# Plain alternation of 512- and 256-column matmuls in every half unit of a two-block kernel

## The reference

```python
h = rms_norm(x, ln_pre_g[layer])
proj = jnp.einsum('bsd,de->bse', h, w_in[layer])                # 2048 -> 18432
rnn_x, rnn_gate, q, k, v, attn_gate, g_rnn, g_attn = split_columns(proj)
hr = rg_lru(rnn_x, ...)                                         # convolution, two gates, scan
y_rnn = jnp.einsum('bsc,cd->bsd', hr * jax.nn.silu(rnn_gate), w_rnn_out[layer])
...                                                             # three dilated groups of 8 heads
y_attn = jnp.einsum('bsc,cd->bsd', o * jax.nn.silu(attn_gate), w_attn_out[layer])
merged = jax.nn.sigmoid(g_rnn) * y_rnn + jax.nn.sigmoid(g_attn) * y_attn
x = x + rms_norm(jnp.einsum('bsd,de->bse', merged, w_o[layer]), ln_post_g[layer])
# second block, for each of two layers:
u = _rmsnorm(x, g_pre) @ w_in                                   # A, B, C inputs and gate logits
...                                                             # o_a, o_b, o_c: 8 heads each
y = sum(gates[:, :, n] * (branches[n] @ w_branch[n]) for n in range(3))
x = x + y @ w_out
```

## Time and profile before

| | |
|---|---|
| median of three runs | 3122.81 us |
| profiled execution, device time | 3123.54 us |
| its span from first to last instruction | 3121.6 us |
| mean granted share of PE's clock | 0.998 |
| PE busy | 3100.0 us, 99% |
| weight loads busy | 2732.4 us, 88% |
| DVE, ACT busy | 68%, 56% |
| chain of waits: share on PE | 98% |
| transfers | 570 MB, 183 GB/s |

### The profile page before, as it was taken

How to read it: one execution, slowest core, us unless ns; L and a number is a source line. 1 busy time by engine, 2 the same in 40 slices (tenths; PEclk the granted TensorE clock), 3 DMA queues, 4 the chain that set the end, 5 groups by cost and what they waited for, 6 DMA issues and landing times.

```text
span 3121.6 us, 52176 instructions
## 1 busy us (share of the span) xinstructions
PE 3100.0 (99%) x18230; PEld 2732.4 (88%) x18230; DVE 2129.6 (68%) x2741; ACT 1734.3 (56%) x2291; POOL 0.2 (0%) x4
## 2 busy tenths in 40 slices
PE   8999999999999899999999999999999999999999
PEld 7888888888888789888888888888888888888888
DVE  7677575766667687766766656777776676665675
ACT  5685444444445556656565555645665656555563
POOL 0000000000000000000000000000000000000000
PEclk9999999999999999999999999999999999999999
DMA  7656665555556565565556666566556555665555
GB/s 230 197 171 202 200 190 169 187 180 172 179 174 211 174 176 159 158 203 173 177 172 194 189 182 182 183 205 185 159 158 203 173 177 172 194 189 183 181 183 180
DMA packets 569809, 571.67 MB, mean 183 GB/s; under 512 B 26352, under 2 KB 565488, under 8 KB 569712
## 3 DMA queue, kind: packets, MB, share of 16 engines
q1 hardware_dynamic: 569712, 570.42, 59.3%
HBM read 568.25 MB, written 2.10 MB: 183 GB/s over the span
## 4 chain that ended last, share of the span: by engine, by line
PE 98%; DVE 1%; ACT 1%; issue 0%; DMA 0%; SPq 0%; ACTq 0%; DVEq 0%
PE pg L544 92%; PE pa L783 1%; PE pa L800 1%; PE pa L544 1%; PE pa L790 1%; PE pa L759 1%; PE pa L801 1%; PE pa L716 0%; DVE hl L1288 0%; PE pa L890 0%; DMA raw<-w_in 0%; ACT hl L945 0%; DVE uT L1369 0%; DVE xres L1747 0%; PE pa L739 0%
## 5 line engine op out<-in xcount | busy, mean ns | idle before, releaser
L544 PE MATMUL pg<-hT,hl 128*128 128x512 f32 x11456 | 2003.8, 335 | 0.9 <-DVE hl L1288 0.9
L544 PEld LDWEIGHTS pg<-hT,hl 128*128 128x128 f32 x11456 | 1742.6, 188 | 241.8 <-DVE hl L1288 4.6
L1288 DVE TENSOR_TENSOR hl<-raw,hl 128x1024 fp32r<-128x1024 f32 (+1 forms) x1071 | 1255.6, 1209 | 304.5 <-ACT hl L945 296.2
L945 ACT ACTIVATE hl<-raw 128x1024 fp32r<-128x1024 f32 (+1 forms) x1071 | 1085.4, 1044 | 300.9 <-PE pg L544 278.9
L544 PE MATMUL pg<-uT,hl 128*128 128x256 f32 (+1 forms) x3712 | 631.4, 331 | 16.9 <-DVE uT L1369 7.9
L544 PEld LDWEIGHTS pg<-uT,hl 128*128 128x128 f32 x3712 | 555.7, 189 | 88.4 <-issue 14.8
L953 ACT ACTIVATE corr<-pg 128x512 f32<-128x512 f32 x286 | 170.3, 595 | 820.8 <-PE pg L544 820.8
L544 PE MATMUL pg<-hl,hT 128*128 128x256 f32 (+1 forms) x1792 | 318.7, 337 | 0.0
L544 PEld LDWEIGHTS pg<-hl,hT 128*128 128x128 f32 x1792 | 276.3, 188 | 39.7
L1295 DVE TENSOR_TENSOR work<-pg,corr 128x512 f32<-128x512 f32 (+1 forms) x154 | 105.8, 687 | 294.5 <-ACT corr L953 294.0
L1120 ACT ACTIVATE work<-work,sm 128x256 f32<-128x256 f32 (+3 forms) x144 | 69.3, 482 | 130.3 <-DVE sm L1566 128.3
(11 more groups left out here) (191 smaller groups left out, 1369.3 us busy)
## 6 DMA issues: line engine op xcount, KB each, us to landing
raw<-w_in SPq DMA_DIRECT2D x791, 512.0 KB, 4.7
raw<-w_br SPq DMA_DIRECT2D x96, 512.0 KB, 4.5
raw<-w_out SPq DMA_DIRECT2D x64, 512.0 KB, 4.7
raw<-w_rnn SPq DMA_DIRECT2D x32, 512.0 KB, 4.7
raw<-w_o SPq DMA_DIRECT2D x32, 512.0 KB, 5.2
raw<-w_att SPq DMA_DIRECT2D x16, 512.0 KB, 4.3
raw<-w_uq SPq DMA_DIRECT2D x16, 384.0 KB, 4.0
tab<-tabs SPq DMA_DIRECT2D x5, 896.0 KB, 7.0
```

Of the source, the lines that this page charges most:

```text
L544: return nc.tensor.matmul(out, lhsT, rhs, start=start, stop=stop, skip_group_check=True)
L945: nc.scalar.activation(part(j, 0, h, 0, n), raw[:, bass.ds(j % 2 * UC + a, n)], ACT.Copy)\
L1288: tt(part(j, 1, h, 0, n), raw[:, bass.ds(j % 2 * UC + a, n)], part(j, 0, h, 0, n).bitcast(F32), ALU.subtract).then_inc(lo_done, 1)
```

## The change

The table `SIDE` and its helpers go, and with them the argument `side` (or `sides`) of all functions. `in_order` keeps plain alternation alone. Counted from the code, 368 of the 1072 half units held something of the table that takes effect: 892 side-by-side pieces and 17 wide-first halves. No matmul, weight load, wait, transfer or instruction of another engine is added, taken away or moved past another engine's; only matmuls of the same half unit change places. The form r has one column block, so nothing changes there.

```diff
-            def in_order(ks, subs, side, wide, narrow):
-
-                if RUNS in side and len(ks) == 4 and ks[0] % 8 == 0:
-                    for k in ks:
-                        for s in range(subs):
-                            wide(k, s)
-                    for k in ks:
-                        for s in range(subs):
-                            ins = narrow(k, s)
-                    return ins
+            def in_order(ks, subs, wide, narrow):
+
                 for k in ks:
                     for s in range(subs):
                         wide(k, s)
-                        if k % 8 not in side:
-                            ins = narrow(k, s)
-                    if k % 8 in side:
-                        for s in range(subs):
-                            ins = narrow(k, s)
+                        ins = narrow(k, s)
                 return ins
...
-    "RG": {3: ends(0, 1), 4: ends(1, 0), 7: ends(0, 1), 8: ends(1, 0), 11: ends(0, 1), 12: ends(1, 0), 15: ends(0, 1),
-           16: ends(1, 0), 21: ends(0, 1), 22: AGAIN, 23: ends(0, 1), 24: AGAIN},
...
-                                                4 * q - 4 * h, ALL)
+                                                4 * q - 4 * h)
...
-                            unit(u + n, n, None, at // 2, h3, n in (1, 4), n in (3, 5), halves=halves, side=ALL)
+                            unit(u + n, n, None, at // 2, h3, n in (1, 4), n in (3, 5), halves=halves)
...
-                                 {"A": (ends(4, 0), ()), "B": ((), ()), "C": (ALL, AGAIN)}[kind])
...
```

More of the change, by code:

```diff
@@ L89 @@
     "C": events("u0-4 norm u5-6 s0-1 x0-1 u7-9 p0 u10 lo0 p1 lo1 u11"),
-}
[L94 to L104, removed]
-    "RG": {3: ends(0, 1), 4: ends(1, 0), 7: ends(0, 1), 8: ends(1, 0), 11: ends(0, 1), 12: ends(1, 0), 15: ends(0, 1),
-           16: ends(1, 0), 21: ends(0, 1), 22: AGAIN, 23: ends(0, 1), 24: AGAIN},
[L107 to L113, removed]
 }
@@ L576, in feature_major, with token_major @@
                                     stop and k == ks[-1]))
-            def token_major(b, hiw, both, op, ks, start, stop, base, side):
+            def token_major(b, hiw, both, op, ks, start, stop, base):
                 return in_order(
-                    ks, 2, side,
+                    ks, 2,
                     lambda k, s: mm(pg3[:, b + s, :], op[:, k, s * P:s * P + P], both[k - base], start and k == ks[0], False),
@@ L618, in opening, with unit @@
                             summed()
-            def unit(u, j, c, cj, op, first, last, form="f", subs=2, ready=None, halves=(0, 1), first_parts=None, side=()):
+            def unit(u, j, c, cj, op, first, last, form="f", subs=2, ready=None, halves=(0, 1), first_parts=None):
                 base = 0 if first else 8
@@ L640, in unit, with product @@
                         if form == "r":
-                            ins = feature_major(b, subs, wh[h], wl[h], op, ks, begin, end, base + 4 * h, side)
+                            ins = feature_major(b, subs, wh[h], wl[h], op, ks, begin, end, base + 4 * h)
                         elif form == "t":
-                            ins = token_major(b, wh, both_view(j, CH), op, ks, begin, end, base, side)
+                            ins = token_major(b, wh, both_view(j, CH), op, ks, begin, end, base)
                         else:
-                            ins = feature_major(b, subs, wh, wl, op, ks, begin, end, base, side)
+                            ins = feature_major(b, subs, wh, wl, op, ks, begin, end, base)
                     ins.then_inc(half_done, 1)
-            def product(u0, c0, op, ready, by_bank=False, sides=((), ())):
+            def product(u0, c0, op, ready, by_bank=False):
                 chunks = NCH // 2 - by_bank
@@ L654, in product @@
                             unit(u0 + 4 * i + 2 * j + k, k, c0 + 2 * i + j, j, op, k == 0, k == 1,
-                                 ready=(lambda ks: ready(ks[0] // 4)) if j == 0 else None,
-                                 side=sides[j] if k == 0 else ())
+                                 ready=(lambda ks: ready(ks[0] // 4)) if j == 0 else None)
                 if by_bank:
@@ L679, in h_split, with half_product @@
                 return lambda q: pe.wait_ge(h_ready, 4 * n + q + 1)
-            def half_product(u0, c0, count, sides=((), ())):
+            def half_product(u0, c0, count):
                 with pe.Fori(0, NCH // 2) as i:
@@ L685, in half_product @@
                         unit(u0 + 2 * i + j, j, c0 + 2 * i + j, j, u3, True, True, form="k",
-                             ready=lambda ks: pe.wait_ge(u_ready, count - 7 + ks[-1]), side=sides[j])
+                             ready=lambda ks: pe.wait_ge(u_ready, count - 7 + ks[-1]))
             def post_sum():
@@ L862, in pair @@
                         is_v = (kind == "1" and 6 <= cc < 9) or (kind in "BC" and cc == 2)
-                        unit(u + n, n, c + cc, cc, h3, n % 2 == 0, n % 2 == 1, "t" if is_v else "f", halves=halves,
-                             side=SIDE[kind].get(n, ()))
+                        unit(u + n, n, c + cc, cc, h3, n % 2 == 0, n % 2 == 1, "t" if is_v else "f", halves=halves)
                     elif what == "norm":
@@ L895, in _ @@
             half_product(U_YA, C_YA, 2 * PAIRS)
-            product(U_WO, C_WO, h3, lambda q: pe.wait_ge(mix_ready, 1 + q), by_bank=True,
-                    sides=((), AGAIN))
+            product(U_WO, C_WO, h3, lambda q: pe.wait_ge(mix_ready, 1 + q), by_bank=True)
             post_sum()
```

14 lines of the change are left out of this document (6 added, 8 removed).

## The result

The changed kernel takes **3132.78 us** in the median of 7 runs (3130.52 to 3135.34), the kernel before 3123.01 (7 runs, 3122.51 to 3123.48). The ratio is 1.0032, with a 95% interval of 1.0021 to 1.0044: 9.8 us slower. The forecast was 3153, 30 us slower. The sign and the range held; the size was three times too large.

What follows compares the result with a forecast made beforehand. PE's own pace was taken as the bound: 16.7 us saved on pieces, against up to 53 us more if all stretches went slow; at two thirds slow, +29.8 us on 3122.81 gives 3153, range 3112 to 3179.

Steps and rivals of the forecast that it cites:

- What bounds the kernel: Whole span: PE is busy 99% and waits only 17.8 us, so time is the sum of PE's own steps.
- The two paces and their price: Alternating halves: 2.72 us fast or 2.80 slow (340 or 350 ns a pair); the slow pace persists after an interruption.
- The share of slow stretches: Stretches behind blocks or waits: two thirds taken as slow, each tenth worth 7.0 us, break-even at 24%.
- the prediction's own sum: Whole kernel: -16.7 + 2/3 x (53 + 16.7) = +29.8 us on the median, giving 3153.
- the pieces' own cost: All side-by-side pieces and wide-first halves: removing them saves 16.7 us if alternation were fast everywhere.
- about a third slow: Rival: only the float32 blocks of one kind, say, go wrong, time 3117 to 3141; chance 0.14.
- The three places it named: Gate product to first values, first block's next pairs, behind B's and C's last weighted values: chunks 11.2 instead of 10.87.
- That branch A's halves would stay at 2.80: Branch A's halves: expected to stay at about 2.80 us each if the forecast was right.
- Waits: PE waiting for DVE, nearest in branch C's output product: 0.6 us margin loses 0.09 to 0.15 but holds; taken as nothing.

Runs made afterwards that it cites:

- the second profile: The changed kernel executed and profiled once more with nothing altered, to see which stretches draw their pace anew: 3137.19 us.
- "Few": Kernel before with its table cut to few pieces and wide-first halves, only where the changed kernel was slow or varied: 3113.75 us, ratio 0.9969.
- The run with the pieces ahead: Kernel before with its table cut to pieces directly ahead of float32 blocks, none behind, plain alternation elsewhere: 3138.01 us, ratio 1.0047.

## Why the prediction was off, step by step

*What bounds the kernel: right.* PE is 99% busy and the waits that the profile lists moved by 0.6 us in all.

*The two paces and their price: right.* The slow stretches show 395 and 280 to 281 ns and 11.19 to 11.20 a chunk, stretches at the fast pace 10.87, and no third pace of alternation appeared. 24 halves gone slow cost 1.92 and 32 cost 2.56, which is 0.08 each. The order mattered, and no stretch ran at the 325 ns a pair that the prediction worked out from the Trainium skill (page "TensorE: Matmul & The Clock Gate", section "Back-to-back issue gap", which gives its formula for an isolated matmul): the fastest alternating pair in any kernel here takes 340.

*The share of slow stretches: the step that failed.* The prediction took two thirds. Of the 753 half units of forms f and k that hold no float32 block and ran at one of the two paces in the changed kernel, 262 were slow (2.79 to 2.81), **35%**; in the second profile 315 of 752, 42%. Put into the prediction's own sum these shares give -16.7 + 0.35 x 69.7 = +7.7 and -16.7 + 0.42 x 69.7 = +12.6, against measured spans of +7.9 and +13.7. So that one factor carried nearly all of the error of 20 us. That the sum then comes so close is luck in part, since two terms are off and offset each other: 262 slow halves cost 262 x 0.08 = 21.0, not 0.35 x 69.7 = 24.4, and the pieces' own cost was nearer 14 than 16.7, as is shown below. The time lay in the rival "about a third slow", which had 0.14.

*Why two thirds was too much.* It was argued that the float32 blocks throw the pairs out at least as much as waits do, from one kind of block. That kind is fast in the changed kernel in both layers: the halves behind it take 2.72, where they took 2.80 with a piece on either side. So a piece behind a block does not always bring the fast pace, and those two entries said nothing of the block without pieces. Each kind of block has an outcome of its own, which its loop repeats. Slow in every pass of both profiles are the halves behind the first block's first transposes and its weighted values, and behind B's first scores, second transposes and second weighted values; in three cases of four those behind the rotation ahead of A's first pair (L881). Fast are, among others, those behind the gates, the first block's second scores, B's first weighted values, all of C's blocks and nearly all of A's. Counted so, seven of some 22 kinds are slow, a third, and not the half of the entries at waits (two and two). A slow stretch between two blocks lasts only to the next block of a fast kind. The blocks are not all of it: about half of the slow halves, 127 of 262, follow a wait or a pause.

*The three places it named.* The first block's next pairs: slow as forecast in three passes of four. The gate product to the first values: fast in one profile, slow from a wait in its 49th half on in the other. Behind B's and C's last weighted values: fast, a miss. That branch A's halves would stay at 2.80 was a miss too: they became fast, 35.41 to 34.85 a pair. In place of these the two w_out products went slow, 5.1 us, behind the pause of 0.2 us in branch C's output product; the prediction had priced the wide-first halves there as mere cost and not as what sets the pace back, and had taken nothing for a wait there.

*The pieces' own cost: a little too large.* "Few" is 9.9 us of span below the kernel before. It still has 26 slow halves (2.1 us) and, by its list, 13 wide-first halves and 32 single pieces (13 x 0.09 + 32 x 0.019 = 1.8 us). Without both it would be 13.8 below, not 16.7; waits that grew are in the 13.8.

*Waits: put at nothing, and one of them began a slow stretch.* The prediction named branch C's output product and said that its margin of 0.6 us holds. It did not. By the same reading, the first low part is there at about 2003.64 + 1.18 = 2004.82 in the changed kernel and ACT's copy starts at 2005.25, a margin of 0.43: 0.15 less, as it had reckoned. That is too little, since PE's queue needs the low part before the half ahead has ended (above: 0.51 us ahead was enough, 0.36 was not). The wait itself costs 0.15, the 37 slow halves behind it 37 x 0.08 = 3.0 in each layer. A second wait grew in the second block's first units: the faster halves behind the sums arrive earlier and wait for the low part. Weight loads of PE there, before and after:

```profile
1162.98 10.97 PEld L544 LDWEIGHTS pg<-hT,hl 128*128 128x128 f32 x64 [0.18 <-DVE hl L1288]
```

```profile
1171.98 10.87 PEld L522 LDWEIGHTS pg<-hT,hl 128*128 128x128 f32 x64 [0.47 <-DVE hl L1248]
```

The chunk of the earlier trace rows takes 1183.20 - 1171.86 = 11.34 after and took 11.03 before, so here the fast pace gave its gain of three halves back:

```profile
1171.86 0.60 ACT L913 ACTIVATE corr<-pg 128x512 f32<-128x512 f32 x1 [0.65 <-PE pg L522]
1183.20 0.60 ACT L913 ACTIVATE corr<-pg 128x512 f32<-128x512 f32 x1 [4.38 <-PE pg L522]
```

*What stays open.* What in a block, a wait or a pause decides the pace behind it was not found. The run with the pieces ahead shows that the order in front of the block has a say, to both sides, and the second profile that the pace behind some waits differs from execution to execution. How often each of these does was not measured by place, only seen in the spread of the times: 4.8 us for the changed kernel, 1.0 for the kernel before in the same series.

## What to carry to other kernels

Where an engine is bound by its own pace and that pace has two values which persist, the price of an order is its price per instruction plus the length of what it leaves behind: a single differently ordered piece of 0.02 us can be worth 2 us of the stretch that follows. Put it directly behind what interrupts, read the profile of the bare order to see which places need one, and leave the others out; then read the profile again, since at two places here alternation was slow behind a piece and fast without one. A margin between two engines counts from where the waiting queue needs the signal: here one of 0.36 us was late. Before a share is taken from two or three places that can be seen, weight it by the length of the stretch behind each kind of place, and give the range by kinds, since loops repeat one outcome.

## What the runs showed of the hardware that was not expected

The two paces are exact, 340 and 350 ns for a pair (2.720 and 2.800 a half to the third digit), and one program takes the one or the other at the same place in different executions. In the trace's starts of single instructions, in the changed kernel's first profile, the wide matmul of a fast pair has a weight load 3 ns behind it nearly each time, that of a slow pair 2 or 3 and 5 ns in turn, repeating only every second pair; a slow stretch of the second profile has 3 and 4 in turn. Side-by-side order has two paces as well, 2.793 and 2.827 a half. Form t has none that shows: 2.77 to 2.79 a half in every kernel that alternates. A wait can hide as "issue": the pause in branch C's output product follows the landing of DVE's low part. All of this at a granted clock of 0.998 of full speed in every profile.
